# The pooling branch's running sums and means moved from VectorE to GpSimd, in a two-layer fp32 transformer kernel

## What is computed

```
def trailing_mean_minus_self(x, window):
    c = jnp.cumsum(xf, axis=1)
    c_shift = jnp.pad(c, ((0, 0), (window, 0), (0, 0)))[:, :s]
    counts = jnp.minimum(jnp.arange(1, s + 1, dtype=jnp.float32), float(window))[None, :, None]
    return ((c - c_shift) / counts - xf).astype(x.dtype)

def multiscale_pool_mixer(u_c, pool_w, pool_scale):
    groups = u_c.reshape(bsz, s, N_POOL_GROUPS, G_C)
    pooled = jnp.stack(
        [trailing_mean_minus_self(groups[:, :, gi], w) for gi, w in enumerate(POOL_WINDOWS)], axis=2)
    mixed = jnp.einsum("bsgc,gcd->bsgd", pooled, pool_w)
    return mixed.reshape(bsz, s, W_C) * pool_scale
```

## Time and profile before

| | |
|---|---|
| median of 3 runs | 2606.76 us (2605.73 to 2608.33) |
| the profiled execution, its time | 2606.62 us |
| its span | 2604.8 us |
| PE busy | 2589.8 us, 99% of the span |
| DVE busy | 1711.2 us, 66% |
| ACT busy | 1296.2 us, 50% |
| POOL busy | 146.8 us, 6% |
| granted PE clock | 0.999 of full |

### The profile page before, as it was taken

The page is one execution under the profiler, slowest core; times in us unless marked ns, Lnnn a source line. Parts: engine busy times, 40 slices in busy tenths (PEclk is TensorE's granted clock), DMA queues, the critical chain, the costliest instruction groups (busy, mean ns, idle before and its releaser), DMA issues.

```text
span 2604.8 us, 50531 instructions
## 1 busy us (share of the span) xinstructions
PE 2589.8 (99%) x20233; PEld 2476.1 (95%) x20233; DVE 1711.2 (66%) x2104; ACT 1296.2 (50%) x1579; POOL 146.8 (6%) x106
## 2 busy tenths in 40 slices
PE   9999999999999999999999999999999999999999
PEld 9899899889999999999999999997899999998887
DVE  7677467566645776767674456998776767675444
ACT  6543374464533655555553344444655555554443
POOL 2001200000200200000001222000020000000000
PEclk9999999999999999999999999999999999999999
DMA  8655456556545666666666665655566666666664
GB/s 267 194 162 187 137 179 196 176 161 204 184 140 165 189 199 193 193 194 192 193 194 195 193 195 180 199 195 163 174 197 194 194 193 192 193 192 207 191 193 146
DMA packets 256273, 487.41 MB, mean 187 GB/s; under 512 B 15069, under 2 KB 80629, under 8 KB 255616
## 3 DMA queue, kind: packets, MB, share of 16 engines
q1 hardware_dynamic: 254496, 476.11, 57.9%
q0 software_dynamic: 1488, 9.19, 1.1%
q10 hardware_dynamic: 144, 0.01, 0.0%
HBM read 483.12 MB, written 2.13 MB: 186 GB/s over the span
## 4 chain that ended last, share of the span: by engine, by line
PE 91%; DVE 7%; ACT 1%; POOL 1%; issue 1%; DMA 0%; SPq 0%; DVEq 0%; ACTq 0%; POOLq 0%
PE ps L2059 90%; DVE w_lo L1296 3%; DVE acc L1806 2%; POOL sumsq L720 1%; DMA raw<-in_weights 0%; ACT w_hi L780 0%; DVE ua L1324 0%; DVE ya L1870 0%; DVE x_res L2040 0%; DVE ub L1324 0%; DVE rstd L1343 0%; PE ps L2580 0%; PE ps L2368 0%; DVE da_sq L1570 0%; DVE y_lo L1351 0%
## 5 line engine op out<-in xcount | busy, mean ns | idle before, releaser
L2059 PE MATMUL ps<-op,w_hi 128*128 128x256 f32 x10048 | 1719.6, 277 | 1.4 <-DVE op L1359 0.8
L1296 DVE TENSOR_TENSOR w_lo<-raw,w_hi 128x1024 fp32r<-128x1024 f32 x899 | 1115.5, 1243 | 815.1 <-ACT w_hi L780 813.5
L2059 PEld LDWEIGHTS ps<-op,w_hi 128*128 128x128 f32 x10048 | 1515.3, 188 | 5.9 <-issue 3.4
L780 ACT ACTIVATE w_hi<-raw 128x1024 fp32r<-128x1024 f32 x899 | 949.4, 1059 | 1094.8 <-PE ps L2059 1047.3
L2059 PE MATMUL ps<-op,w_lo 128*128 128x256 f32 x5024 | 1387.4, 276 | 0.0
L2059 PEld LDWEIGHTS ps<-op,w_lo 128*128 128x128 f32 x5024 | 943.2, 188 | 0.0
L2059 PE MATMUL ps<-g,w_hi 128*128 128x256 f32 x1408 | 239.4, 276 | 0.0
L2059 PE MATMUL ps<-w_hi,g 128*128 128x512 f32 x704 | 218.9, 392 | 0.0
L2059 PEld LDWEIGHTS ps<-g,w_hi 128*128 128x128 f32 x1408 | 211.7, 188 | 0.0
L2059 PE MATMUL ps<-g,w_lo 128*128 128x256 f32 x704 | 194.3, 276 | 0.0
L2059 PE MATMUL ps<-w_hi,op 128*128 128x512 f32 x512 | 165.3, 397 | 0.0
(11 more groups left out here) (300 smaller groups left out, 1396.3 us busy)
## 6 DMA issues: line engine op xcount, KB each, us to landing
raw<-in_weights SPq DMA_DIRECT2D x899, 512.0 KB, 4.4
x_res<-in_x SPq DMA_DIRECT2D x8, 256.0 KB, 5.4
mem_x<-in_mem POOLq DMA_DIRECT2D x1, 2048.0 KB, 8.5
x_res<-in_x POOLq DMA_DIRECT2D x1, 2048.0 KB, 10.3
w_row<-row_dram POOLq DMA_DIRECT2D x2, 1024.0 KB, 7.4
out_x<-x_res SPq DMA_DIRECT2D x3, 512.0 KB, 2.8
rel_rev<-rel_dram POOLq DMA_DIRECT2D x1, 1024.0 KB, 8.2
hg_con<-in_hg_consts POOLq DMA_DIRECT2D x1, 576.0 KB, 5.3
```

Source lines behind the costliest of these rows:

```text
L780: nc.scalar.activation(w_hi[:, s], raw[:, s], ACT.Copy).then_inc(hi_rounded, 1)
L1296: TT(w_lo[:, s], raw[:, s], w_hi[:, s].bitcast(F32), ALU.subtract).then_inc(chunk_split, 1)
L2059: return nc.tensor.matmul(out, lhsT, rhs, start=start, stop=stop, skip_group_check=True)
```

## The change

POOL gets the three steps of the pooling work, in the same order and on the same buffers, right after the start of the pool_w load. It waits for dve_evac, that is, for px. It waits for its own instruction's end between the dependent steps; the eight products have no wait among them, nor have the four subtractions. DVE keeps the reading of px, loses the sums and means, and takes three taps in each of slots 6 to 15 (30 in place of 24). The list of taps is as long as before, so it is empty six taps earlier.

```
--- before.py
+++ after.py
@@ -758,6 +758,24 @@
             pool.wait_ge(chunk_used, GM["down"].end_chunk)
             pool.dma_start(pw[:, :, :], A["pool_w"]).then_inc(pool_w_loaded, 16)
 
+            pad = lambda buf, lo, back: buf[:, lo:4, PPAD - back:PPAD - back + TOK]
+            pool.wait_ge(dve_evac, GM["pool"].end_evac)
+            for n in range(4):
+                src, dst = (px, pa, pb, pa)[n], (pa, pb, pa, pb)[n]
+                if n:
+                    steps.wait()
+                steps.inc(TT(pad(dst, n, 0), pad(src, n, 0), pad(src, n, 1 << n), ALU.add))
+            steps.wait()
+            for n in range(4):
+                s = (pa if n % 2 == 0 else pb)[:, n, PPAD:PPAD + TOK]
+                steps.inc(TT(s[:, 0:PPAD], s[:, 0:PPAD], cc("inv_count", n * PPAD, PPAD), ALU.mult))
+                steps.inc(nc.gpsimd.tensor_scalar(s[:, PPAD:TOK], s[:, PPAD:TOK], 1.0 / WINDOWS[n], None, ALU.mult))
+            steps.wait()
+            for n in range(4):
+                s = (pa if n % 2 == 0 else pb)[:, n, PPAD:PPAD + TOK]
+                ins = TT(s, s, px[:, n, PPAD:PPAD + TOK], ALU.subtract)
+            ins.then_inc(pool_made, 1)
+
             pool.wait_ge(std_ready, STD_END[4])
             pool.wait_ge(rows_stored, 16)
             pool.wait_ge(operand_ready, READY["pool"] + 2)
@@ -1827,25 +1845,6 @@
                         both(at_slot(SLOTS, lambda: conf_out(2)), at_slot(SLOTS + 1, lambda: conf_glu(2)),
                              lambda k: some_taps(4) if k > 5 else None))
 
-            pad = lambda buf, lo, back: buf[:, lo:4, PPAD - back:PPAD - back + TOK]
-
-            def window_sums(n):
-
-                src, dst = (px, pa, pb, pa)[n], (pa, pb, pa, pb)[n]
-                steps.inc(TT(pad(dst, n, 0), pad(src, n, 0), pad(src, n, 1 << n), ALU.add))
-                steps.wait()
-
-            def pool_means():
-                for n in range(4):
-                    s = (pa if n % 2 == 0 else pb)[:, n, PPAD:PPAD + TOK]
-                    steps.inc(TT(s[:, 0:PPAD], s[:, 0:PPAD], cc("inv_count", n * PPAD, PPAD), ALU.mult))
-                    steps.inc(TS(s[:, PPAD:TOK], s[:, PPAD:TOK], 1.0 / WINDOWS[n], None, ALU.mult))
-                steps.wait()
-                for n in range(4):
-                    s = (pa if n % 2 == 0 else pb)[:, n, PPAD:PPAD + TOK]
-                    ins = TT(s, s, px[:, n, PPAD:PPAD + TOK], ALU.subtract)
-                ins.then_inc(pool_made, 1)
-
             def gated_out(b):
 
                 g = GM["gated"]
@@ -1906,14 +1905,8 @@
                     if k == 4:
                         take(GM["pool"], lambda b, i: px[:, 2 * i:2 * i + 2, PPAD:PPAD + TOK], 1)(0, 0, GM["pool"].first_block % 2)
                         take(GM["pool"], lambda b, i: px[:, 2 * i:2 * i + 2, PPAD:PPAD + TOK], 1)(0, 1, GM["pool"].first_block % 2)
-                    if k == 5:
-                        dve.wait_ge(dve_evac, GM["pool"].end_evac)
-                    if 5 <= k < 9:
-                        window_sums(k - 5)
-                    if k == 9:
-                        pool_means()
-                    if k > 9:
-                        some_taps(4)
+                    if k > 5:
+                        some_taps(3)
                 if b and k == 4:
                     gated_out(b - 1)
                 if b == 1:
```

## The result

| | before | with the change |
|---|---|---|
| median of 20 runs each | 2606.48 us | 2609.92 us |
| the profiled execution | 2606.62 us | 2610.29 us |
| its span | 2604.8 us | 2608.5 us |
| POOL busy | 146.8 us | 165.8 us |

The ratio of the times is 1.0013, with a 95% interval of 1.0007 to 1.0019: the changed kernel is 3.4 us slower, between 1.8 and 5.0 us. The forecast was 2612.4 us, 0.2% slower. The direction and the mechanism were right; the forecast rise was 5.6 us, the measured one 3.4 us. The measured time lies under the 2611 to 2614 us that the prediction gave to its own main case, and among the times of its rival "shorter holds".

A forecast was written before the change was run, and what follows sets the result against it. DVE, without lead until out_2's chunk 6, was taken to bound the kernel: 9.15 us of POOL's holds against 3.59 us of relief adds 5.6 us to 2606.62, giving 2612.2, forecast as 2612.4 us; range 2606.0 to 2618.0 us.

The forecast's parts named there:

- main case: Whole kernel: the forecast of 2612.4 us, 0.2% slower, with times from 2611 to 2614 us; chance 0.50.
- shorter holds: Rival: POOL's small instructions cost DVE little, holds sum to 6 to 8 us, about 2610 us; chance 0.23.
- What bounds the kernel: DVE, from px to out_2's chunk 6: a microsecond more DVE work ahead of 1785.9 is a microsecond at the end.
- The moved work, 5.96 less and 2.37 more: DVE loses sums and means, 5.96 us, and gains six earlier taps, 2.37 us: 3.59 us less.
- The ACT gate: Split at 1707.11: ACT's rounding ends at 1706.62, so DVE cannot be earlier there by more than 0.5 us.
- the rival without exclusion: Holds in slots 5 to 15 under 3.6 us relieve DVE, but gain only 0.5 us: 2606.3 us; chance 0.07.
- The kind of the hold: Slots 5 to 15: POOL and DVE take turns; a POOL add stops DVE's next instruction about its time less 0.2 us.
- The size of the holds, 9.15 us: POOL's instructions hold DVE: adds 5.55 us, subtractions 2.2, products of 16 columns 0.4, tensor_scalar 1.0; sum 9.15 us.
- PE's waits, 9.3 us: PE's waits for DVE's splits grow from 3.7 to about 9.3 us, as out_2's chunk 6 split comes 5.6 us later.
- POOL's chain, ending near 1701: POOL's instructions from 1676.3: 15.4 us alone plus 9.3 waiting for DVE; no wait of PE for pool_made expected.

The follow-up runs named there:

- POOL's work without relief: Kernel before, DVE keeping all its work, plus the change's sixteen POOL instructions, writing two buffers nobody reads: 2613.24 us, ratio 1.0029.
- the relief alone: Changed kernel without POOL's sixteen instructions; sums, means and subtractions left out, PE's pool_mix reads px itself: 2605.85 us, ratio 0.9997.
- the kernel with taps as before: Changed kernel with no taps in slots 5 to 9 of gated block 0 and four in each of slots 10 to 15: 2606.86 us, ratio 1.0003.
- the means alone: Kernel before with only the products and subtractions on POOL, the four adds and the taps staying on DVE as before: 2606.50 us, ratio 1.0001.
- the 35 adds: Changed kernel plus 35 POOL adds on POOL's own buffer, output unread, during the product out: 2618.41 us started at 574.6 us, 2610.92 us at 604.7.
- late taps: Six taps of out_2's slots 4 and 5 moved behind the split PE waits for: 2604.28 and 2604.64 us on kernel before, 2605.79 on changed kernel.

## Why the prediction was right, and where its size was off

- **What bounds the kernel.** Right. DVE is busy with next to no gap from the px reading on, and its delay reaches PE at chunk 6 of out_2 1:1. POOL's work without relief cost 6.9 us at the end, against 6.8 us of longer DVE instructions in the changed kernel's trace.
- **The moved work, 5.96 less and 2.37 more.** Right. The ACT gate, which the rival without exclusion named, was right too: the relief alone gave 0.5 us, as worked out there, not 3.6.
- **The kind of the hold.** Right: an add of POOL stops DVE's taps and splits, and DVE's stop POOL's. The Trainium skill (SBUF — State Buffer, "Who interferes with whom") says that two such instructions contend, and that the contention is an exclusive lock. The trace agrees for the adds and subtractions, and not for the products: a tensor_scalar took 1.02 us, and DVE's rows beside it grew by 0.19 us at most.
- **The size of the holds, 9.15 us.** This step failed; it was 6.7 to 6.8. The adds were put at 5.55 us and held 4.2. Their rate came from sums of squares, whose inputs lie far apart; the inputs of the first three pooling adds lie 1 to 4 elements apart, and such adds take a fifth less time on POOL. If the hold shrinks alike, that makes 4.6 us (2304 elements at 2.17 x 1.0/1.24 ns and 256 at 2.17); the remaining 0.4 stays open. The eight products were put at 1.4 us and held 0.6. The subtractions were put at 2.2 and held 2.0. With 6.8 in place of 9.15 the sum gives 3.2 us in place of 5.6, against 3.4 measured. The rival "shorter holds", with a chance of 0.23, had this range, 6 to 8 us. Its reason, that small instructions cost DVE little, fits the products; for the adds, the larger part of the error, the reason was another one. That 2609.9 us lies inside the range owes much to the width of the range, 12 us, which took in the case of no hold as well.
- **PE's waits, 9.3 us.** They were 5.6. Smaller holds explain 2.4 us of the difference; the rest is mostly that the sum took the list of waits for their cost, and short waits are listed shorter than they are.
- **POOL's chain, ending near 1701.** It ended at 1696.0. Cheaper adds explain about 1 us of the difference; the rest is that the sixteen instructions waited for DVE far less than the 9.3 us of the sum (the first for 2.2 us, no other for more than about 0.8). PE reached pool_mix at 1703.1. No wait for pool_made, as said.

## What to carry to other kernels

Before work goes to GpSimd, look at the lead of VectorE in that stretch. Where VectorE has idle time, GpSimd's holds land in it and cost little; where VectorE feeds PE without a gap, they are paid for in full. Here the four adds, about 5.2 us of GpSimd's time without the first one's wait, held VectorE for 4.2 us, and the subtractions, about 3.5 us, for 2.0. Work that took VectorE less than that is a loss. Do not fill the freed slots of VectorE while GpSimd is still at work, and look at ACT first: four scalings there took 0.4 us each beside VectorE's taps without touching them. More than half of what was gained in the end, 1.6 to 1.9 of 2.9 us, came from another place, six taps moved behind the one split that PE waits for.

## What the runs showed of the hardware that was not expected

- The time of a two-input add on GpSimd depends on the distance of its inputs: 0.98 to 1.01 us for 484 to 492 columns at 1 to 4 elements, 1.22 to 1.26 us for 476 to 496 columns at 8, 16 and 512.
- GpSimd and VectorE do not take strict turns. The first pooling add waited through both splits of slots 5 and 6 and took 3.93 us, of which some 1.8 us (an estimate) lie behind the end of the second split at 1679.0. In the kernel with taps as before it took 5.06 us, through three splits in a row. In the changed kernel no later one waited through more than one of VectorE's instructions. Why the first waits longer stays open; the runs do not tell.
- The same wait on PE was followed by the half clock in some traces and not in others. Ten traces hold a wait of 2.82 to 2.85 us ahead of chunk 6 of out_2. In six of them, those of both kernels among them (0.61 of full over 3 us before, 0.73 over 4 us from 1789 us with the change), the granted clock fell behind it. In four it stayed at 1.00: without POOL's work, with the means alone, and with the 35 adds started at 574.6 and at 604.7 us. After the wait of 1.4 us, with late taps, it stayed at 1.00 in all four traces. The ten traces are of ten kernels, one each, so what decides stays open. The times suggest that it changes from one execution to the next: twenty executions of the kernel before spread over 3.9 us (2604.4 to 2608.3), eleven with late taps over 1.7 us (2603.4 to 2605.0). A median of such executions is a mixture, and a difference of 1 us or so between two of them can come from the clock alone.
